# A decode kernel whose selected-cache pages get a third place in the spilled residual's region

## The reference, cut to what matters

```python
def nsa_core(q, q_pos, kc_blk, vc_blk, gather_sel, n_sel_blocks, kvw, kw_pos):
    s_c = jnp.einsum('bqgrd,bngd->bgrqn', q, kc_blk) * scale
    p_c = masked_softmax(s_c, blk_end[None, :] <= q_pos[:, None])
    o_c = jnp.einsum('bgrqn,bngd->bqgrd', p_c.astype(dt), vc_blk)
    imp = p_c.sum(axis=2)
    ...
    _, idx = lax.top_k(score, min(N_SEL, n_sel_blocks))
    kv_g = gather_sel(idx)
    ...
    s_s = jnp.einsum('bqgrd,bgqnkd->bgrqnk', q, kv_g[..., 0, :]) * scale
    o_s = jnp.einsum('bgrqnk,bgqnkd->bqgrd', p_s.astype(dt), kv_g[..., 1, :])
    s_w = jnp.einsum('bqgrd,bkgd->bgrqk', q, kvw[:, :, 0]) * scale
    o_w = jnp.einsum('bgrqk,bkgd->bqgrd', p_w.astype(dt), kvw[:, :, 1])
    return o_c, o_s, o_w

def layer_update(x, mq, mg, mem_kv, mix, zg, w_out_i):
    y = jnp.concatenate([jax.nn.silu(mg) * mem_attend(mq, mem_kv), jax.nn.silu(zg) * mix], axis=-1)
    return x + y @ w_out_i
```

## Time and profile before

| | |
|---|---|
| median of three runs | 1040.93 us (1040.17 to 1042.69) |
| the profiled execution's own time | 1036.34 us |
| its span, first to last instruction | 1034.7 us |
| mean granted TensorE clock | 0.982 |
| TensorE busy | 965.7 us, 93% of the span |
| sample stage (front(0) to the last copy) | about 804 to 964 us |
| output projection and final norm | about 964 us to the end |

### The profile page before, as it was taken

The page is one execution under the profiler, slowest core; times in us unless marked ns, Lnnn a source line. Parts: engine busy times, 40 slices in busy tenths (PEclk is TensorE's granted clock), DMA queues, the critical chain, the costliest instruction groups (busy, mean ns, idle before and its releaser), DMA issues.

```text
span 1034.7 us, 17598 instructions
## 1 busy us (share of the span) xinstructions
PE 965.7 (93%) x6530; PEld 600.6 (58%) x6530; DVE 599.1 (58%) x1356; ACT 298.2 (29%) x734; POOL 70.6 (7%) x133
## 2 busy tenths in 40 slices
PE   5999999999977999999999999989899899998997
PEld 3576676667754445566755555665555666655443
DVE  3204997797543645999914222448876667766113
ACT  4310010100143023112124221347776434435012
POOL 0000000000000000000012010310000222120000
PEclk9999999999988999999999999999999999999999
DMA  8543644554361443386522351453002878774202
GB/s 350 184 101 123 174 122 143 172 161 100 107 206 42 104 141 123 92 212 193 181 82 101 104 185 53 162 218 109 40 1 97 312 239 301 278 247 164 103 2 90
DMA packets 48879, 153.03 MB, mean 148 GB/s; under 512 B 9497, under 2 KB 23194, under 8 KB 41882
## 3 DMA queue, kind: packets, MB, share of 16 engines
q1 hardware_dynamic: 43674, 135.13, 40.8%
q0 software_dynamic: 5120, 16.78, 4.7%
HBM read 142.26 MB, written 17.89 MB: 155 GB/s over the span
## 4 chain that ended last, share of the span: by engine, by line
PE 78%; DVE 8%; DMA 6%; issue 4%; ACT 1%; POOLq 1%; SPq 1%; POOL 0%; DVEq 0%; ACTq 0%
PE PS L1275 70%; PE PS L1278 8%; DMA arena<-in_csel 4%; DVE arena L2190 1%; DVE arena L2396 1%; DMA arena<-in_wall 1%; POOLq L589 1%; DMA arena<-in_cmem 1%; DVE arena L2001 1%; POOL arena L590 0%; DVE arena L2033 0%; DVE arena L2034 0%; ACT arena L1188 0%; DVE arena L2401 0%; SPq L589 0%
## 5 line engine op out<-in xcount | busy, mean ns | idle before, releaser
L1275 PE MATMUL PS<-arena 128*32 128x64 f32 (+16 forms) x5436 | 833.3, 376 | 21.7 <-issue 7.4
L1275 PEld LDWEIGHTS PS<-arena 128*128 128x128 f32 (+6 forms) x5436 | 478.2, 148 | 348.1 <-issue 220.7
L1278 PE MATMUL PS<-arena 128*128 128x128 f32 (+3 forms) x1094 | 150.4, 285 | 39.7 <-ACT arena L898 11.0
L1278 PEld LDWEIGHTS PS<-arena 128*128 128x128 f32 (+3 forms) x1094 | 125.1, 146 | 78.0 <-issue 40.2
L2033 DVE TENSOR_TENSOR arena<-arena 128x2048 f32<-128x2048 f32 x32 | 73.2, 2288 | 3.6 <-DMA arena<-in_ccmp 2.4
L2034 DVE TENSOR_TENSOR arena<-arena 128x2048 f32<-128x2048 f32 x32 | 73.1, 2285 | 0.0
L1051 ACT ACTIVATE arena<-arena 128x512 f32<-128x512 f32 (+3 forms) x96 | 53.0, 555 | 30.1 <-DVE arena L2190 30.0
L2190 DVE CUSTOM_DVE_ANT_0 arena<-PS,arena 128x512 f32<-128x512 f32 (+3 forms) x96 | 41.5, 487 | 20.6 <-PE PS L1275 20.6
L590 POOL DMA_DIRECT2D arena<-in_csel x64 | 34.7, 541 | 209.4 <-PE PS L1278 99.2
L2294 DVE TENSOR_TENSOR arena<-arena,PS 128x512 f32<-128x512 f32 x16 | 11.0, 687 | 57.0 <-PE PS L1275 56.9
L2036 DVE TENSOR_TENSOR arena<-arena 128x1024 f32<-128x1024 f32 x32 | 39.0, 1219 | 0.0
(11 more groups left out here) (207 smaller groups left out, 560.9 us busy)
## 6 DMA issues: line engine op xcount, KB each, us to landing
arena<-in_wall SPq DMA_DIRECT2D x19, 2048.0 KB, 9.6
arena<-in_ccmp SPq DMA_DIRECT2D x128, 256.0 KB, 3.7
arena<-in_csel POOLq DMA_DIRECT2D x64, 256.0 KB, 5.6
arena<-in_csel SPq DMA_DIRECT2D x64, 256.0 KB, 5.1
arena<-in_cmem SPq DMA_DIRECT2D x32, 256.0 KB, 6.1
arena<-in_win SPq DMA_DIRECT2D x8, 1024.0 KB, 9.3
out_win_s<-in_win SPq DMA_DIRECT2D x1, 8064.0 KB
x_scratch<-arena SPq DMA_DIRECT2D x1, 2560.0 KB, 9.3
```

The lines of the kernel that those rows point to most:

```text
L1275: return nc.tensor.matmul(out, lhsT, rhs, start=start, stop=stop, skip_group_check=True)
L1278: return nc.tensor.transpose(out, in_, ident[0:in_.shape[0], 0:in_.shape[0]])
```

## The change: a third place for two quarters, and another order of loads

The residual is not loaded back during prompt attention. Its region gives quarters 1 and 2 a third place: in that region the quarters 1 and 2 of sequence 1 are loaded during prompt attention, and those of sequence 4 later. The residual is loaded back before the loads of the last sequence, after back(4). In the last sequence quarters 1 and 2 therefore take the place that sequence 5 had, not that of sequence 4. Quarter 0 keeps three places in another order, quarter 3 keeps two, elsewhere. In each turn both lists now load quarters 1 and 2 of t, quarter 0 of t + 1, then (SP) the window of t, then quarter 3 of t. Quarters 1 and 2 share a semaphore, and TensorE waits at quarter 1 for both. Weight block 19 is loaded ahead of block 18, after back(5).

```diff
--- before.py
+++ after.py
@@ -364,12 +364,27 @@
         def four_pages(a):
             return a.rearrange("p (s c) -> p s c", s=4)
 
-        FIRST = [four_pages(a) for a in (at(8192, 2048), at(4096, 2048), shared)]
-        LATER = [[four_pages(at(o, 2048)) for o in quads] for quads in ((10240, 0, 2048), (12288, 14336, 16384))]
+        PAGES = [[four_pages(a) for a in quads] for quads in (
+            (at(8192, 2048), shared, at(4096, 2048)),
+            (at(10240, 2048), arena[:, 0:2048], at(12288, 2048)),
+            (at(0, 2048), arena[:, 2048:4096], at(14336, 2048)),
+            (at(2048, 2048), at(16384, 2048)))]
+
+        def place(t, c):
+
+            return 2 if t == NB - 1 and c in (1, 2) else t % len(PAGES[c])
+
+        def last_in(t, c):
+
+            return max([s for s in range(t) if place(s, c) == place(t, c)], default=None)
+
+        def times(t, c):
+
+            return sum(place(s, c) == place(t, c) for s in range(t + 1))
 
         def skv(t, c):
 
-            return LATER[t % 2][c - 1] if c else FIRST[t % 3]
+            return PAGES[c][place(t, c)]
 
         SWKT = at(18432, 1024).rearrange("p (g c) -> p g c", g=2)
         SM = at(19456, 2112)
@@ -469,8 +484,9 @@
             sem("pc_" + n) for n in ("scored", "shifted", "probs", "normed", "p_turned", "copied")]
         blk_zero = sem("cmp_blocks_zero")
         fut_set = sem("future_set")
-        sa_lo = [[sem(f"sa_pages01_{c}_{n}") for n in range(2 if c else 3)] for c in range(4)]
-        sa_hi = [[sem(f"sa_pages23_{c}_{n}") for n in range(2 if c else 3)] for c in range(4)]
+        sa_lo, sa_hi = [[[sem(f"sa_pages{h}_{c}_{n}") for n in range(len(PAGES[c]))] for c in (0, 1, 3)] for h in ("01", "23")]
+        sa_lo.insert(2, sa_lo[1])
+        sa_hi.insert(2, sa_hi[1])
         (sa_cs, sa_cm, sa_ce, sa_cn, sa_imp, sa_mask, sa_ft, sa_fa, sa_fd, sa_s, sa_m, sa_p,
          sa_bt, sa_ba, sa_bd, sa_used, sa_mix, sa_y, sa_done) = [
             sem("sa_" + n) for n in ("cmp_scored", "cmp_max", "cmp_exp", "cmp_normed", "imp",
@@ -582,13 +598,13 @@
 
         def quad_load(eng, t, c, pages, loaded):
 
-            places = 2 if c else 3
-            if t >= places:
-                eng.wait_ge(sa_used, START.sa_used + 6 * (t - places) + c + 2)
+            last = last_in(t, c)
+            if last is not None:
+                eng.wait_ge(sa_used, START.sa_used + 6 * last + c + 2)
             for s in pages:
                 page = eng.value_load(ptab[0:1, NPG * t + 4 * c + s:NPG * t + 4 * c + s + 1], min_val=0, max_val=POOL - 1)
                 eng.dma_start(skv(t, c)[:, s, :], I["csel"][bass.ds(page, 1), :, :].rearrange("a p c -> (a p) c")
-                              ).then_inc(loaded[c][t % places], 16)
+                              ).then_inc(loaded[c][place(t, c)], 16)
 
         def sample_phase(front, middle, back):
 
@@ -741,7 +757,8 @@
             quad_load(sp, 0, 0, range(2), sa_lo)
             quad_load(sp, 0, 1, range(2), sa_lo)
             sp.wait_ge(cp_took, NB + 1)
-            sp.dma_start(Xf, x_dram).then_inc(x_back, 16)
+            quad_load(sp, 1, 1, range(2), sa_lo)
+            quad_load(sp, 1, 2, range(2), sa_lo)
             sp.wait_ge(pa_t, BANKS_OF_P * (UNITS - 2))
             quad_load(sp, 0, 2, range(2), sa_lo)
             sp.wait_ge(pa_t, BANKS_OF_P * (UNITS - 1))
@@ -749,21 +766,26 @@
             sp.wait_ge(pa_s, PT * UNITS)
             window(0)
             sp.wait_ge(pa_mix, 6)
+            sp.wait_ge(state_out, 16)
             quad_load(sp, 1, 0, range(2), sa_lo)
+            quad_load(sp, 1, 3, range(2), sa_lo)
             window(1)
-            for t in range(1, NB):
-                for c in range(1, 4):
-                    quad_load(sp, t, c, range(2), sa_lo)
+            quad_load(sp, 2, 0, range(2), sa_lo)
+            for t in range(2, NB):
+                if t == NB - 1:
+                    sp.wait_ge(sa_used, START.sa_used + 6 * (NB - 3))
+                    sp.dma_start(Xf, x_dram).then_inc(x_back, 16)
+                quad_load(sp, t, 1, range(2), sa_lo)
+                quad_load(sp, t, 2, range(2), sa_lo)
                 if t + 1 < NB:
-                    if t == 1:
-                        sp.wait_ge(state_out, 16)
                     quad_load(sp, t + 1, 0, range(2), sa_lo)
-                    window(t + 1)
-
+                window(t)
+                quad_load(sp, t, 3, range(2), sa_lo)
+
+            sp.wait_ge(sa_used, START.sa_used + 6 * (NB - 2))
+            load_w(B_OUT1 + 1)
             sp.wait_ge(sa_used, START.sa_used + 6 * (NB - 1))
             load_w(B_OUT1)
-            sp.wait_ge(sa_used, START.sa_used + 6 * (NB - 1) + 2)
-            load_w(B_OUT1 + 1)
             sp.wait_ge(sz_done, 1)
             sp.dma_start(gfin, I["gfin"]).then_inc(gfin_in, 16)
             for t in range(TT):
@@ -856,20 +878,25 @@
             pool.wait_ge(sig_done, SILUS)
             quad_load(pool, 0, 0, range(2, 4), sa_hi)
             quad_load(pool, 0, 1, range(2, 4), sa_hi)
+            pool.wait_ge(cp_took, NB + 1)
+            quad_load(pool, 1, 1, range(2, 4), sa_hi)
+            quad_load(pool, 1, 2, range(2, 4), sa_hi)
             pool.wait_ge(pa_t, BANKS_OF_P * (UNITS - 2))
             quad_load(pool, 0, 2, range(2, 4), sa_hi)
             pool.wait_ge(pa_t, BANKS_OF_P * (UNITS - 1))
             quad_load(pool, 0, 3, range(2, 4), sa_hi)
             pool.wait_ge(pa_mix, 6)
+            pool.wait_ge(state_out, 16)
+            pool.wait_ge(gates_written, 16)
             quad_load(pool, 1, 0, range(2, 4), sa_hi)
-            for t in range(1, NB):
-                for c in range(1, 4):
-                    quad_load(pool, t, c, range(2, 4), sa_hi)
+            quad_load(pool, 1, 3, range(2, 4), sa_hi)
+            quad_load(pool, 2, 0, range(2, 4), sa_hi)
+            for t in range(2, NB):
+                quad_load(pool, t, 1, range(2, 4), sa_hi)
+                quad_load(pool, t, 2, range(2, 4), sa_hi)
                 if t + 1 < NB:
-                    if t == 1:
-                        pool.wait_ge(state_out, 16)
-                        pool.wait_ge(gates_written, 16)
                     quad_load(pool, t + 1, 0, range(2, 4), sa_hi)
+                quad_load(pool, t, 3, range(2, 4), sa_hi)
 
 
         @block.scalar
@@ -1866,9 +1893,9 @@
                     k = TURNED[j]
                     if k < 8:
                         if k % 2 == 0:
-                            places = 2 if k else 3
-                            pe.wait_ge(sa_lo[k // 2][number % places], 32 * (number // places + 1))
-                            pe.wait_ge(sa_hi[k // 2][number % places], 32 * (number // places + 1))
+                            c, loads = k // 2, 64 if k // 2 in (1, 2) else 32
+                            pe.wait_ge(sa_lo[c][place(number, c)], loads * times(number, c))
+                            pe.wait_ge(sa_hi[c][place(number, c)], loads * times(number, c))
                         for q in range(2):
                             for g in range(2):
                                 ins = turn(PS[:, FRONT_BANK[j], 256 * q + 128 * g:256 * q + 128 * g + 128],
```

## The result

The changed kernel took 1059.74 us (median of 4 runs, 1056.62 to 1061.32), beside 1041.81 (4 runs) for the kernel before. The ratio is 1.0166, with an interval of 1.0133 to 1.0199. Slower, as forecast, but by 17.9 us where the forecast had 5.9, and outside its range.

What follows compares the result with a forecast made beforehand. TensorE, busy 93% of the span, was taken as the bound, with 7.3 us of page waits to gain. Terms -1.28 + 1.46 + 2.82 - 1.63 + 3.10 + 1.4 gave +5.9 us: median 1046.8, range 1037 to 1055.

Steps and rivals of the forecast that it cites:

- j = 6 and then at j = 8: Turns in a front's transposes: TensorE would wait for the window before the first, for quarter 3's pages before the second.
- its signs: What would show it right: window and page waits in fronts 2 to 5, steps near 19.8, longest step at t = 7.
- t = 7: Last sequence: sixteen pages all wait for back(5); step 21.71 for 18.61, +3.10, plus +1.4 for a clock drop.
- The four steps of t = 2 to 5: Times between starts of successive backs' values: 19.83 us each, +1.46 for t = 2 and three times +0.94.
- Start of the loads: SP's first page of a turn (moment T) leaves 2.0 us after the values of back(t-2) begin (moment V).
- Landing of SP's eighth page: The last needed page, of quarter 3, lands 14.1 us after the first page leaves (T).
- the bounds: Landing after T: 12.4 us if only twelve needed pages come first, 15.4 if both queues share evenly and sixteen go by.
- the one stretch with the order in question: Earlier trace from 804.83 with the new order by chance: the fourth page lands at T + 14.5.
- Release to new V: From TensorE's release by quarter 3's page to the start of the next back's values: 3.73 us.
- the third rival: Clock falls in each front with even sharing: +11.1, or +16.7 (1057.6) if idle costs 1.4 each; chance 0.18 beyond +10.
- Front(1) and t = 6: Front(1) loses its wait, -1.28; in t = 6 no wait is left, 18.23 for 19.86, -1.63, keeping the gap of 1.00.
- The rival that the waits go: Window and quarter 3 land by V + 13.5, so fronts 1 to 6 do not wait: -1.9 to -6.4; chance 0.16.

Runs made afterwards that it cites:

- run 1: The changed kernel with the window of t sent ahead of the wait for quarter 0 of t+1: 1037.34 us, ratio 0.9984 to the kernel before.
- run 2: The changed kernel with POOL holding back its early quarters 1 and 2 until the window of the sequence before theirs has landed: 1042.10 us, ratio 1.0034.
- run 3: The changed kernel with extra identity transposes keeping TensorE busy ahead of the waits for the window and quarter 3: 1050.74 us, ratio 1.0122.
- runs 4 to 6: Three kernels with the third place but the old load order, differing in when the residual's reload and weight blocks leave: 1044.45, 1037.64 and 1040.56 us.
- run 5: Against run 4: all eight sequences take the three places in turn, and the residual's reload leaves after back(7) has used quarter 2: 1037.64 us, ratio 0.9959.
- run 8: Run 1's order, with all eight sequences taking the three places in turn and the reload after back(7) has used quarter 2: 1029.33 us, ratio 0.9897.
- run 4: The changed kernel's places in the old load order, with the residual's reload right after the last sequence's pages: 1044.45 us, ratio 1.0041.

## Why the prediction was right or wrong

**Direction and mechanism: right.** The window behind the wait for quarter 0 of t+1 was named as the cost, and run 1 shows that the place of this one line is the whole loss. The waits came where they were forecast, at j = 6 and then at j = 8, in t = 2 to 5. Of its signs one failed: the longest steps are t = 2 to 5, not t = 7.

**The four steps of t = 2 to 5: too small, 4.3 us where 22.3 were measured.** Two terms of the sum were mis-sized and one hardly:
- Start of the loads: 2.0 taken, 2.14 measured.
- Landing of SP's eighth page: T + 14.1 taken, T + 16.4 measured, 2.3 a step. The choice between the bounds went wrong: it followed the one stretch with the order in question, and went a little below it. All of POOL's pages took their share, as run 2 shows by holding them back. Even the upper bound of 15.4 was short; it came from pages alone, while a window lies among these sixteen page sizes, but no run shows that this is the reason.
- Release to new V: 3.73 taken, 5.8 measured (mean of 6.39, 5.85, 5.39 and 5.55), 2.1 a step. The step that failed here is the sentence that the clock costs "nothing in t = 2 to 5, where the wait splits into two parts below 2 us". The parts were 0.85 and 2.80, 3.56 and 1.22, 3.88 and 0.56, 2.18 and 2.46, and the clock fell to 0.50 in all four; run 3 gives it back. With the landing 2.3 later one part was bound to be longer than forecast, so this error follows in part from the one before.

Added up, 0.14 + 2.3 + 2.1 is 4.5 a step and 18 in four, which is the whole difference between forecast and measurement in these steps. It is the third rival (even sharing and the clock in each front, 1057.6 forecast) that happened, and it was given too little. That its 1057.6 lies so near the 1059.74 measured is in part luck: it is +16.7 for a profiled execution, where +23.7 was measured. The profiled execution of before was a fast one, 4.6 below the median of three runs and 5.5 below that of the four beside the changed kernel, so by medians the loss is 17.9.

**Front(1) and t = 6: right.** The wait of front(1) is gone (-1.3), and t = 6 gave -1.3 for -1.63, though by another way: the gap of 1.00 that the forecast kept did not come, and a wait of 1.03 for the window, which it did not have, stood in its place.

**t = 7: the size nearly right, the place wrong.** 21.84 us measured for 21.71 and 1.4 of clock. The last page of quarter 3 landed at 960.30, T + 15.3 where 15.4 was taken, and TensorE came to it just behind that. But the wait stood elsewhere: 3.02 us at the first turn of quarter 1, where quarter 2 was to be late by "under 1 us", and then none for the window or for quarter 3. Quarters 1 and 2 share a semaphore, so TensorE waited for eight pages at once; the last of them, POOL's second page of quarter 2, left at 949.17 and landed at 956.14, and TensorE went on at 956.28. The half clock came behind this wait, but by these times it cost the step little, because the slow transposes ran while quarter 3 was still under way: the 1.4 was one term too many.

**The rival that the waits go** asked for the window and quarter 3 by V + 13.5. In t = 3 the window came at V + 15.6 and quarter 3 at V + 18.5. With the window sent in time (run 1) fronts 1 to 5 lost their waits, and front(6) kept 0.99 us.

**Open.** The gaps without a releaser in runs 4 to 6 (1.72 to 2.54 us, in the values) were not settled. The traces of all ten kernels agree on one thing: from the first values on, there are 37 such gaps of 0.36 us and more in TensorE's products (scores and values, not the transposes) up to 990 us, and TensorE goes on from each of them 2.2 to 2.9 us after a transfer of 16 KB on the queue for instructions (q8) began; in run 5 it began at 885.85, and TensorE went on at 888.38. The seven longest are all in runs 4 to 6. There the DMA engines' busy share was 0.89 to 1.09 in the 1.5 us before that transfer and 0.13 to 0.54 in the 2.5 us after its start, so it began as the loads ran out. In back(3) it began 0.8 and 0.95 us behind V in runs 1 and 8 (gaps of 0.76 and 0.92), and 2.35 to 2.5 us behind V in runs 4 to 6 (gaps of 2.25 to 2.30). That would fit instructions that come late behind loads, but no run was made that takes the loads away at that moment, so the cause is not shown.

Of run 8's gain over run 1 (8 us by the medians, 7.2 between the profiled executions) 3.9 us lie between the first V and the last, 3.45 of them in t = 7 (21.46 to 18.01). Another 1.65 lie ahead of the first V, and 1.6 behind the last one, in the output projection (71.9 and 70.2 us). These two are no larger than what separates executions of nearly the same program there: the first V stands between 824.2 and 828.9 us in the changed kernel and runs 1, 2, 3 and 8, and the projection takes 72.0 us in the changed kernel and 70.3 in run 3.

## What to carry to other kernels

When loads are reordered on a queue that also waits, ask of each load when its own place comes free, and put it ahead of every wait that ends later: a load that could have left a sequence earlier cost about 22 us here by standing one line too low (1059.74 against 1037.34 in run 1, on two chips). When a bound depends on how two queues share, take the even share if the other queue has anything to send, and allow for the clock when TensorE is idle for several us, also when the idle time comes in two pieces. Let big loads that nobody needs soon leave last, behind the small ones that somebody waits for.

## What the runs showed of the hardware

- Idle time in two pieces can bring the granted clock to 0.50: it was 0.50 over the 6.8 us of the rows above behind 0.85 and 2.80 us, 3.56 and 1.22, 3.88 and 0.56, and 2.18 and 2.46, and cost about 2.1 us of work, in the mean of the four. "TensorE: Matmul & The Clock Gate" of the Trainium skill, section "What's actually happening", says that the gate is set by how busy TensorE has been recently; these four rows agree.
- The length of the idle time alone did not decide it. In run 1 the clock stayed at 1.00 behind pieces of 2.52 and 1.22 us. In run 2 it stayed there behind 1.1 to 1.9 us in one piece, and was 0.65 behind 2.24. In the last back, behind the same wait for ScalarE, 19 transposes took 3.64 us in the kernel before (idle 3.14) and 2.29 in the changed kernel (idle 3.15).
- A page of 256 KB on POOL's queue, which landed in 6.3 and 7.3 us beside other pages, took 8.7 beside the reload (2560 KB) and a weight block (2048 KB) on SP's in run 4, and 9.0 beside the reload in run 1. It is not always so: in the changed kernel one that left 0.2 us ahead of the reload took 7.4.
- Sixteen page sizes with a window among them released TensorE 16.0 to 16.8 us after the first page left, where the last of sixteen pages had landed after 14.9 and 15.8.
- The longest gaps in TensorE's products without a releaser (1.72 to 2.54 us, runs 4 to 6) ended 2.4 to 2.6 us after a 16 KB transfer on the queue for instructions began, and that transfer began as the loads ran out.
